# One decoder layer on one core: the preparation dissolved into the first group's steps

## The reference

```python
u = rmsnorm(x, pre_mix_gain)                 # per token, over 1024 features
proj = u @ w_in                              # 1024 x 3080: x, g, q, k, v, o of 512 columns each, and 8 gate columns
rg:  conv4(x) -> two block-diagonal gates -> h_t = a_t h_(t-1) + b_t -> * gelu(g) -> rmsnorm
ml:  silu(conv4(q)), silu(conv4(k)), v, chunkwise mLSTM over 4 heads
     log_i = ml_i + igate_b ;  log_f = log_sigmoid(ml_f + fgate_b)      # the 8 gate columns
     bcum = cumsum(log_f) in a chunk ; m = running max over chunks of (b_last + m, m_loc)
     decay matrix, weights and the floor of the denominator follow from bcum, log_i and m
h = x + rmsnorm(concat(y_rg, y_ml) @ w_out)
out = h + rmsnorm(relu(rmsnorm(h) @ w_up)^2 @ w_down)
```

## Time and profile before

| | us |
|---|---|
| median of 3 runs | 2471.45 |
| the profiled execution | 2468.74 |
| its span, first to last instruction | 2467.1 |
| PE's first mixer unit begins, in the trace | 139.33 |
| PE's unit q of step 4 (the first of group 1) begins | 295.95 |

### The profile page before, as it was taken

One profiled execution on the slowest core, in us unless ns is written; L12 is line 12 of the kernel. 1 busy time (PEld: TensorE's weight loads), 2 busy tenths in 40 slices (PEclk: granted clock), 3 DMA queues, 4 the chain that ended last, 5 costly groups with the idle time before them and its releaser, 6 DMA issues.

```text
span 2467.1 us, 30099 instructions
## 1 busy us (share of the span) xinstructions
PE 2332.6 (95%) x10696; PEld 1940.3 (79%) x10696; DVE 1268.0 (51%) x1584; ACT 642.5 (26%) x1159; POOL 964.3 (39%) x550
## 2 busy tenths in 40 slices
PE   5679999999998698999999999989899999999998
PEld 5668888888887587888888888868688888888886
DVE  5345665756666255345435444517655434534535
ACT  3314544545546242001101101114211101100112
POOL 8400000000000208658457555620757546644830
PEclk7589999999999799999999999989999999999999
DMA  5634544645542542111111111327312111111103
GB/s 171 259 130 126 170 168 140 198 141 165 176 145 71 172 160 77 52 52 60 43 43 60 43 43 51 102 92 252 133 52 69 43 40 53 51 35 50 60 26 145
DMA packets 124888, 253.80 MB, mean 103 GB/s; under 512 B 8072, under 2 KB 43104, under 8 KB 124832
## 3 DMA queue, kind: packets, MB, share of 16 engines
q1 hardware_dynamic: 96720, 156.32, 18.9%
q0 software_dynamic: 24320, 88.35, 11.2%
q10 hardware_dynamic: 3792, 8.47, 0.9%
HBM read 200.62 MB, written 50.40 MB: 102 GB/s over the span
## 4 chain that ended last, share of the span: by engine, by line
PE 62%; POOL 2%; DMA 1%; issue 0%; DVE 0%; ACT 0%; POOLq 0%; SPq 0%; PEldq 0%; ACTq 0%; DVEq 0%
PE o_ps L1358 21%; PE o_ps L1360 21%; PE o_ps L1359 21%; POOL w_lo L1329 1%; POOL w_hi L1327 1%; POOL o_w_raw L1309 0%; PE o_ps L1382 0%; DMA o_v_lo<-ylo_d 0%; DMA o_w_raw<-in_w_out 0%; POOL o_w_lo L1329 0%; DVE o_acc L1572 0%; DVE o_v_lo L1627 0%; DVE o_acc L1578 0%; ACT o_v_hi L1502 0%; DVE o_acc L1648 0%
## 5 line engine op out<-in xcount | busy, mean ns | idle before, releaser
L1358 PE MATMUL o_ps<-o_v_hi,w_hi 128*128 128x512 f32 x1024 | 401.6, 392 | 12.9 <-POOL w_lo L1329 8.0
L1327 POOL TENSOR_TENSOR w_hi<-o_w_raw,one 128x1024 fp32r<-128x1024 f32 x100 | 205.1, 2051 | 514.6 <-PE o_ps L1360 509.4
L1359 PE MATMUL o_ps<-o_v_lo,w_hi 128*128 128x512 f32 x1024 | 400.5, 391 | 0.0
L1360 PE MATMUL o_ps<-o_v_hi,w_lo 128*128 128x512 f32 x1024 | 400.3, 391 | 0.0
L1648 DVE TENSOR_TENSOR o_acc<-o_ps,o_acc 128x512 f32<-128x512 f32 x224 | 153.3, 690 | 370.2 <-PE o_ps L1360 370.2
L1634 DVE TENSOR_TENSOR o_relu<-o_relu 128x512 f32<-128x512 f32 x128 | 232.6, 1817 | 189.3 <-ACT o_relu L1513 188.2
L658 PE MATMUL m_unit_ps<-u_hi,w_hi 128*128 128x512 f32 x768 | 308.8, 402 | 6.3 <-issue 6.3
L1513 ACT ACTIVATE o_relu<-o_ps 128x512 f32<-128x512 f32 x128 | 76.4, 597 | 863.9 <-PE o_ps L1360 831.7
L658 PE MATMUL m_unit_ps<-u_hi,w_lo 128*128 128x512 f32 x768 | 301.0, 392 | 0.0
L658 PE MATMUL m_unit_ps<-u_lo,w_hi 128*128 128x512 f32 x768 | 299.4, 390 | 0.0
L1329 POOL TENSOR_TENSOR w_lo<-o_w_raw,w_hi 128x1024 fp32r<-128x1024 f32 x102 | 267.7, 2625 | 47.2 <-ACT w_hi L1528 39.4
(11 more groups left out here) (256 smaller groups left out, 3746.9 us busy)
## 6 DMA issues: line engine op xcount, KB each, us to landing
o_w_raw<-in_mlp_w_up POOLq DMA_DIRECT2D x64, 512.0 KB, 4.6
o_w_raw<-in_mlp_w_down POOLq DMA_DIRECT2D x64, 512.0 KB, 3.5
u_hi<-uhi_d SPq DMA_DIRECT2D x14, 2048.0 KB, 10.5
u_lo<-ulo_d SPq DMA_DIRECT2D x14, 2048.0 KB, 15.0
w_raw<-in_w_in POOLq DMA_DIRECT2D x24, 512.0 KB, 4.9
p_xu<-in_x SPq DMA_DIRECT2D x16, 512.0 KB, 7.8
uhi_d<-u_hi SPq DMA_DIRECT2D x4, 2048.0 KB, 7.4
ulo_d<-u_lo SPq DMA_DIRECT2D x4, 2048.0 KB, 13.1
```

The costliest lines, as they stand in the source:

```text
L1327: pool.tensor_tensor(w_hi[i], w_raw[i % 2][:], one_bc, ALU.mult).then_inc(w_split[i], 1)
L1358: nc.tensor.matmul(dst, sh, mh, start=(i == 0), stop=False)
L1359: nc.tensor.matmul(dst, sh, ml, start=False, stop=False)
L1360: last = nc.tensor.matmul(dst, sl, mh, start=False, stop=(i == n - 1))
```

## The change

`build_prepare` is gone. What it did is done inside `build_mixers`, in the steps p = 0 to 3 of the first group, whose PE, ACT, DVE and SP streams are now written out step by step instead of in a loop:

- Block t of 512 tokens is loaded (`load_x`), squared (`squares`), scaled by the inverse root alone (`scale_x`, the gain comes with the evacuation as a per-partition scale), transposed (`transpose_x`: 8 feature tiles of four 128x128 transposes) and split into high (`high_of_x`, ACT) and low (`low_of_x`, DVE, reading PSUM). Block 0 is done ahead of step 0. Block p+1 is done in step p: squares before the copy of q, the scaling between the queries' convolution and the values' weighting, the transposes two by two behind the units v, x, o and g.
- The tiles of x of the blocks 1 to 3 use the three raw weight tiles (and one more tile); so block 1 is loaded when the six weight tiles of the first group have been split, and a later block when the transposes of the one before are done.
- The 8 gate columns are a seventh unit (`gate_unit`), ahead of q, with 24 matmuls of 8 output rows by 512 columns. ACT copies its result with the bias (`copy_gates`), POOL sends it to DRAM and reads it back as 16 rows (4 heads by 4 chunks) of 128 (`gate_rows`), and the chain of small instructions runs per block on those 16 rows: `gate_absolute`, `gate_exponential`, `chunk_locals`, `chunk_maxima`, `chunk_rows`, with PE's transposes (`chain`) behind the units x, o and g and ACT's `floor_columns` at the end. The maximum is carried from block to block in `m_carry`.
- Blocks 0 to 3 of u are stored for the later groups from there (`store_u`). The rows of a block are stored and loaded at the end of its step (`load_rows`), where the kernel before loaded them a step ahead. The gate weights of the RG-LRU are loaded from the input with four DMAs in each step instead of one from SBUF.
- The first POOL work is now the identity and the loads of the first three weight tiles.

```diff
-def build_prepare(nc, a, k):
...
-            build_prepare(nc, a, k)
...
+        def x_tile(t, i):
+            if t == 0:
+                return x_first[i][:]
+            if i == 3:
+                return x_extra[:]
+            return w_raw[i][:].rearrange("p k f -> p (k f)")
...
+        gap_tiles = {2: (0, 1), 3: (2, 3), 4: (4, 5), 5: (6, 7)}
...
+            def load_x(t):
+                if t == 1:
+                    for u in "xog":
+                        sp.wait_ge(w_split[u], 2)
+                elif t:
+                    sp.wait_ge(x_tr, KT * t)
+                for i in range(CPT):
+                    sp.dma_start(x_tile(t, i), a["x"][0, (t * CPT + i) * P:(t * CPT + i + 1) * P, :]).then_inc(x_in[i], 16)
...
+            load_x(0)
+            store_u(0)
+            load_x(1)
             load_rows(0)
-            with sp.Fori(0, STEPS // 2 - 1) as j:
+            load_x(2)
+            store_u(1)
+            load_rows(1)
+            load_x(3)
...
+            def gate_rows(t):
+
+                pool.wait_ge(if_copied, t + 1)
+                pool.dma_start(k["gates_d"][t], gate_sb[:]).then_inc(gates_out, 16)
+                pool.wait_ge(gates_out, 16 * (t + 1))
+                for h, row in enumerate((li_row, lf_row)):
+                    pool.dma_start(row[:], k["gates_d"][t, h * NG:(h + 1) * NG].rearrange("g (c p) -> (g c) p", p=P)
+                                   ).then_inc(gates_in, 16)
...
+            for t in range(NT - 1):
+                gate_rows(t)
+            pool.wait_ge(x_tr, KT * NT)
...
+            def transpose_x(t, c):
+                pe.wait_ge(scaled, CPT * (t + 1))
...
+            def gate_unit(p):
+                pe.wait_ge(ulo_made, KT * (p + 1))
...
+            def chain(p, n):
+                ident = k["ident"][0:RB, 0:RB]
+                if n == 3:
+                    pe.wait_ge(locals_made, p + 1)
...
+                if n == 4:
+                    pe.wait_ge(if_copied, p + 1)
+                    pe.wait_ge(prev_made, p + 1)
...
+                if n == 5:
+                    pe.wait_ge(rows_made, p + 1)
...
+            for p in range(NT):
+                gate_unit(p)
+                for n, u in enumerate(UNITS):
+                    unit(u, p, p % 2)
+                    if p:
+                        slots[n](p - 1)
+                    chain(p, n)
+                    if p < NT - 1:
+                        for c in gap_tiles.get(n, ()):
+                            if c == 5:
+                                pe.wait_ge(ulo_made, KT * (p + 1) + 4)
+                            transpose_x(p + 1, c)
...
                 if mix:
                     sigmoids_1(m)
+                if gates:
+                    copy_gates(p)
+                if prepare:
+                    squares(p + 1)
                 if project:
                     take("q")
                 if mix:
                     sigmoids_2(m, g_m)
+                if prepare:
+                    root_x(p + 1)
...
+            def scale_x(t):
+                dve.wait_ge(squared, CPT * (t + 1))
...
+                dve.wait_ge(std_made, t + 1)
+                link(nc.vector.reciprocal(rstd[:], std[:]))
+                for i in range(CPT):
+                    tile = x_tile(t, i)
+                    nc.vector.tensor_scalar(tile, tile, rstd[:, i:i + 1], None, ALU.mult).then_inc(scaled, 1)
+
+            def low_of_x(t, c):
+                dve.wait_ge(uhi_made, KT * t + c + 1)
+                nc.vector.scalar_tensor_tensor(out=u_lo[:, t % 2, c, :], in0=tr_bank(t, c), scalar=gain(c),
+                                               in1=u_hi[:, t % 2, c, :].bitcast(F32), op0=ALU.mult, op1=ALU.subtract
+                                               ).then_inc(ulo_made, 1)
+
+            def gate_absolute(p):
+                dve.wait_ge(gates_in, 32 * (p + 1))
...
+                if gates:
+                    gate_absolute(p)
+                if project:
                     convolve("q", p, g_p)
                 if mix:
                     gate_input(m)
                     gelu_2(m)
+                if prepare:
+                    scale_x(p + 1)
+                if mix:
                     weigh_values(m)
                     weigh_scores(m)
                     weigh_queries(m)
                 low_of("q")
                 if project:
                     convolve("k", p, g_p)
+                if gates:
+                    chunk_locals(p)
                 if mix:
                     one_minus_a2(m)
                     states(m)
+                low_parts_x(2)
+                if mix:
                     recurrence(m)
                 low_of("k")
                 if mix:
                     head_numerator(m)
                 low_of("v")
+                low_parts_x(3)
                 if project:
                     convolve("x", p, g_p)
                     keep_history(p)
+                if gates:
+                    chunk_maxima(p)
+                low_parts_x(4)
                 if mix:
                     rg_output(m, g_m)
                     head_total(m)
                     head_output(m)
                 low_of("x")
+                if gates:
+                    chunk_rows(p)
                 if mix:
                     rg_square_sums(m)
                     rg_low(m)
+                low_parts_x(5)
                 low_of("o")
                 low_of("g")
```

More of the change, by code:

```diff
@@ L510, in build_mixers @@
         gate_w = sb("gate_w", [P, 2, P])
+        hist = sb("hist", [P, 3, 3])
+        with ExitStack() as first:
+            x_first = [first.enter_context(nc.sbuf_tensor(f"m_x_first{i}", [P, D], F32)) for i in range(CPT)]
         xbuf = sb("xbuf", [P, 3, TILE + 3])
-        hist = sb("hist", [P, 3, 3])
         conv = {u: sb("conv_" + u, [P, TILE]) for u in "qkx"}
@@ new lines, in _ @@
+            pool.memset(k["ident"][:], 0.0).then_inc(ident_made, 1)
+            pool.wait_ge(ident_made, 1)
+            pool.affine_select(out=k["ident"][:], in_=k["ident"][:], compare_op=ALU.not_equal, fill=1.0,
+                               base=0, pattern=[[-1, P]], channel_multiplier=1).then_inc(ident_made, 1)
+            for c in range(3):
+                load_first(c)
+            pool.memset(k["one"][:], 1.0).then_inc(const_made, 1)
+            pool.memset(k["mask"][:], BIG).then_inc(const_made, 1)
@@ new lines, in gate_unit @@
+            def gate_unit(p):
+                pe.wait_ge(ulo_made, KT * (p + 1))
+                if p:
+                    pe.wait_ge(rows_made, p)
+                for c in range(KT):
+                    for z, (w, x) in enumerate(((wif_hi, u_hi), (wif_hi, u_lo), (wif_lo, u_hi))):
+                        last = nc.tensor.matmul(n_ps[0:2 * NG, :], w[:, c, :], x[:, p % 2, c, :],
+                                                start=(c == 0 and z == 0), stop=(c == KT - 1 and z == 2))
+                last.then_inc(if_mm, 1)
@@ L737, in _ @@
+            with pe.Fori(0, (STEPS - NT) // 2) as j:
+                for b in range(2):
+                    p = j * 2 + (NT + b)
                     for n, u in enumerate(UNITS):
-                        unit(u, p, b)
+                        unit(u, p, b, j * 32 + 32)
                         slots[n](p - 1)
-            for n, u in enumerate(UNITS):
-                unit(u, STEPS - 1, 1)
-                slots[n](STEPS - 2)
             for slot in slots:
@@ L1083, in low_of, with low_parts_x @@
                         split_low(u, g_p)
+                gates = isinstance(p, int) and p < NT
+                prepare = isinstance(p, int) and p < NT - 1
+                def low_parts_x(n):
+                    if prepare:
+                        for c in gap_tiles[n]:
+                            low_of_x(p + 1, c)
                 if mix:
```

650 lines of the change are left out of this document (274 added, 376 removed), and 9 rows, old and new, of the table base.

## The result

The changed kernel takes 2499.12 us (median of 4 runs, 2497.34 to 2502.5) against 2471.52 for the kernel before: 1.0111 times, 95% interval 1.0099 to 1.0122. It is 1.1% slower, where 2453 was forecast; the time lies outside the stated range of 2425 to 2477. Its profiled execution spans 2496.5 us, and PE is busy for 93% of it.

What follows compares the result with a forecast made beforehand. PE, busy 95% of the span, was taken as the bound, with gains where it idles early: 35 + 58.5 + 62.9 + 62.9 + 56, plus 4 for the clock, gives 279.3 instead of 295.95; 2453 us forecast, range 2425 to 2477.

Steps and rivals of the forecast that it cites:

- The start: Preparation of block 0 before the first gate unit: PE's first gate product at 35 us, bounds 28 to 38.
- The four scalings: VectorE's scaling of block 0 beside POOL's weight splits: 9 us taken, from bounds of 3 to 9.
- Step 0: First step of the first group, from its gate unit on: 58.5 us.
- PE's wait for block 1: In step 0, PE waits 6.6 us for block 1's scaled tiles before its transposes, until 65.0.
- Step 1: Second step of the first group: 62.9 us, 11.3 over PE's own work.
- the three waits drawn: PE's waits in steps 1 and 2: states and low parts behind x, maxima behind o, last low parts at the end.
- The wait for the maxima: In steps 1 and 2, PE waits behind unit o, from T+45.9 to T+48.3, for VectorE's maxima.
- Steps 2 and 3: Last two steps of the first group: 62.9 us for step 2, 56 us for step 3.
- the sum: Start and steps 0 to 3 give 275.3, with 4 for the clock 279.3: 16.7 us won, 2453 forecast.
- the loads of x decide: Rival: x's loads take 13.8 us, making steps 0 to 2 each 6 us longer; 2471, no change; chance 0.12.
- Behind step 4: After the first group: rows late by some 4 us once, inside DVE's slack; three more small DMAs, nothing on the path.
- The clock: PE restarting at half clock after waits over 5 us loses 1.45 us each time; 4 us added to the sum.

Runs made afterwards that it cites:

- experiment 1: Changed kernel with the stores of the recurrence's y of mixer steps 0, 1 and 2 issued ahead of x's load and u's stores and loads: 2461.92 us.
- experiment 2: Changed kernel with only the y store of mixer step 2 moved ahead of the 4 MB load of u, in step 4: 2487.81 us.
- experiment 11: On top of experiment 7, VectorE takes up the rows later, from step 4 on: 2442.8 us.
- experiment 4: Changed kernel with only the two 4 MB loads of u put behind y's stores; x's load and u's stores stay ahead: 2479.8 us.
- experiment 5: Changed kernel with the recurrence's y of steps 0 and 1 stored on GpSimd's queue, the rest of SP's order unchanged: 2470.8 us.
- experiment 7: On top of experiment 1 with the gates taken up later (2454.78 us), the floor and y's low part also come later: 2449.14 us.

## Why the prediction was wrong

*The start* came out at 37.8 us against 35, inside its bounds of 28 to 38, by errors that offset each other. The four scalings took 11.5 us beside POOL's weight splits, over the 9 taken and over the bound: 2.87 us each, where the longest row I had was 2.26. With POOL idle, in step 0, three of the same instructions took 2.08 us, 0.69 each.

```profile
17.83 11.47 DVE L985 TENSOR_SCALAR m_x_first<-m_x_first,m_rstd 128x1024 f32<-128x1024 f32 x4
62.19 2.08 DVE L985 TENSOR_SCALAR w_raw<-w_raw,m_rstd 128x1024 f32<-128x1024 f32 x3
```

*Step 0* took 53.7 us against 58.5; PE's wait for block 1 ended at 64.98, drawn at 65.0. *Step 1* took 64.3 us against 62.9, with two of the three waits drawn: 5.8 us at the numerators for the low parts and 5.0 at the next gate unit. The wait for the maxima did not come. VectorE was busy for 40.1 us of it, drawn at 44.2.

*Steps 2 and 3 failed*, 76.0 us against 62.9 and 76.7 against 56. The step of the working that failed is the wait of ScalarE's stream that it left out: step 2 was given the 62.9 us of step 1 without a look at what ScalarE's first instructions of a step wait for, and behind step 4 the sum says "later steps issue three more small DMAs, nothing on the path". I counted what the new opening of SP adds for the rows and gates, and x's loads as a rival, but did not follow y's store, an old instruction, past the 4 to 8 MB that now stand ahead of it, and did not ask who waits for it. So the square's wait stood at nothing; it was 21.1, 27.9 and 19.7 us, and moving y's stores ahead gave back 37 us (experiment 1). Nor was it in a rival: "the loads of x decide" names the right queue and the wrong victim. x itself was nearly in time: the squares of step 1 waited 2.0 us for it.

Experiment 1 puts only this right and is the test of the rest. Its unit q of step 4 starts at 279.5; the forecast was 279.3. Its steps take 53.8, 63.4, 67.4 and 56.7 us, with 58.5, 62.9, 62.9 and 56 drawn, so the match is partly luck: step 0 was 4.8 too long, the start 3.3 too short and step 2 4.4 too short, and the 4 us added for the clock make up the rest.

*Behind step 4* nothing was to be lost. The changed kernel loses 17.4 us in step 4: 11.3 to y's store (experiment 2); of the rest, experiment 11 finds 3.6, on another base, in VectorE's wait for the rows, which the kernel before had ready long ahead. The remaining 2.5 us are not explained. In experiment 1's kernel gates to gates of this step is 48.7 us against 40.9, 7.8 more, which is why it runs at 2462 and not at 2453.

So the error of 46 us is 37 for the order of SP's DMAs (experiment 1) and 9 for what step 4 loses besides and for the executions' spread. The last line of the sum was also a slip: 2452.1 us and the 2.7 between the profiled execution and the median make 2454.8, not 2453.

*The clock* was priced at 4 us. In the changed kernel PE came back at half clock behind nine waits between 130 and 345 us, all of 3.9 us or more: a product then takes 0.60 us or more, the two of a gate 2.05 for 1.02. It stayed there for 2.9 to 6.2 us, where 3 was taken. PE's busy time in windows of half a microsecond, times the share of the clock that was not granted, comes to 20 us over the nine, 2.3 each where the prediction has 1.45. By the same count experiment 1's kernel loses 13 us between 130 and 316 behind its six. So some 8 of the 37 us went through the clock; the rest is waiting. That experiment 1 nevertheless met the forecast start of step 4 means that most of what its clock cost lay where PE would have waited in any case, or was made up by terms drawn too long; no run here separates the two.

## What to carry to other kernels

When a hand-written order of DMAs is rewritten, list for each queue what now stands ahead of every old transfer, in bytes, and follow who waits for it; a small store that frees a buffer goes ahead of large transfers, or on a queue of its own. A wait at the head of an engine's step delays the whole step: moving one victim ahead of it gave 10 us here, taking most of the wait away 37. Put last in a step what nobody waits for (here the floor with its table load), and count a change of a loop's code only where the code is reached.

## What the runs showed of the hardware that I had not expected

An issue of a DMA on SP took 0.3 to 0.7 us when little stood ahead, but 5.4 and 7.0 us behind 4 to 8 MB (233.25 and 243.76 in the changed kernel): the issuing engine itself stands. What is behind it in its stream is delayed twice, y's low part by 20.3 us until its issue and by 9.8 from there to its landing.

A store of 256 KB landed 2.3 to 2.4 us after its issue in seven of eight cases of the kernel before; first in line with the load of the rows just ahead in 5.8 to 6.7 (experiments 1 and 4); on a second queue, while SP's queue carried 6 and 8 MB, in 8.3 and 6.1 (experiment 5). The DMA engines moved 361 to 366 GB/s by the windows and by the difference of experiment 4.

How long PE stood idle did not by itself decide its clock. Behind waits of 3.9 us and more it came back at half each time between 130 and 345 us, but at the first gate unit it started at full behind 3.18 us in the changed kernel and at half behind 2.40 in experiment 1's (38.27, 0.59 us a product), and behind 1.8 it kept the full clock once and fell to half one product later the other time (experiment 7).
